# Three places in a decoder layer: squares between weight splits, twelve experts ahead in the search, running sums folded before the last group

## The reference, cut to what matters

```python
def _finish(x, mods, conv_raw, attn, ...):
    conv_y = _conv_tail(conv_raw, conv_ln_g, conv_ln_b)
    a = _rmsnorm(attn, attn_out_g)
    mix = jnp.concatenate([conv_y, a], axis=-1) @ w_out
    x = x + (1.0 + mods[2]) * mix
    h = _rmsnorm(x, norm2_g) * (1.0 + mods[4]) + mods[3]
    return x + (1.0 + mods[5]) * _peer(h, peer_wq, peer_keys, peer_u, peer_v)

def _peer(h, wq, keys, u_tab, v_tab):      # per block of tokens
    q = (tb @ wq).reshape(TOK_BLOCK, PEER_HEADS, 2, PEER_DK)
    s = jnp.einsum('thpd,hpkd->thpk', q, keys)
    sv, si = lax.top_k(s, PEER_TOPK)
    cand = sv[:, :, 0, :, None] + sv[:, :, 1, None, :]
    fv, fi = lax.top_k(cand.reshape(...), PEER_TOPK)
    eid = i1 * PEER_NKEYS + i2             # 128 x 128 experts
    g = jax.nn.softmax(fv, axis=-1)
    hid = jax.nn.gelu(jnp.einsum('td,ted->te', tb, u_tab[eid]))
    return jnp.einsum('te,ted->td', g * hid, v_tab[eid])
```

## Time and profile before

| | |
|---|---|
| median of three runs | 2441.48 us (2439.57 to 2441.72) |
| the profiled execution | 2438.12 us |
| its span of instructions | 2436.3 us |
| PE busy | 2257.6 us (93%) |
| PE weight loads busy | 1965.1 us (81%) |
| DVE busy | 1645.2 us (68%) |
| ACT busy | 925.3 us (38%) |
| POOL busy | 355.9 us (15%) |
| chain that ended last | PE 83%, DVE 7%, DMA 6%, ACT 3%, issue 1% |

### The profile page before, as it was taken

The page is one execution under the profiler, slowest core; times in us unless marked ns, Lnnn a source line. Parts: engine busy times, 40 slices in busy tenths (PEclk is TensorE's granted clock), DMA queues, the critical chain, the costliest instruction groups (busy, mean ns, idle before and its releaser), DMA issues.

```text
span 2436.3 us, 38402 instructions
## 1 busy us (share of the span) xinstructions
PE 2257.6 (93%) x14756; PEld 1965.1 (81%) x14756; DVE 1645.2 (68%) x2907; ACT 925.3 (38%) x1034; POOL 355.9 (15%) x316
## 2 busy tenths in 40 slices
PE   7699999767979988999999999999999999999986
PEld 2298888436859988988999888888888888889985
DVE  1259777324345697866888777777877777766775
ACT  0332332342243314634444343343443443444432
POOL 1043000200000004510011212222212222010000
PEclk9899999778989999999999999999999999999999
DMA  9867776766634534576777999888989889877652
GB/s 382 349 234 288 286 277 226 279 242 225 236 127 145 163 131 153 216 250 234 266 273 282 344 345 324 327 338 323 345 307 345 334 319 341 290 275 266 209 176 91
DMA packets 152112, 643.36 MB, mean 264 GB/s; under 512 B 16721, under 2 KB 17105, under 8 KB 133649
## 3 DMA queue, kind: packets, MB, share of 16 engines
q1 hardware_dynamic: 122112, 444.65, 51.8%
q0 software_dynamic: 28400, 187.90, 19.9%
q10 hardware_dynamic: 1440, 8.56, 0.8%
HBM read 618.05 MB, written 22.99 MB: 263 GB/s over the span
## 4 chain that ended last, share of the span: by engine, by line
PE 83%; DVE 7%; DMA 6%; ACT 3%; issue 1%; POOL 0%; SPq 0%; DVEq 0%; ACTq 0%
PE vb L1429 17%; PE zb L1412 15%; PE vb L1431 7%; PE zb L1414 7%; PE zb L481 6%; PE zb L483 6%; PE zb L482 6%; DMA ada_first<-in_w_ada 3%; PE zb L1374 3%; PE vb L1452 3%; PE vb L1441 2%; PE vb L1394 2%; PE vb L1102 2%; DMA cache<-in_cv 1%; PE vb L1428 1%; DVE lo L465 1%
## 5 line engine op out<-in xcount | busy, mean ns | idle before, releaser
L456 ACT ACTIVATE hi<-raw 128x1024 fp32r<-128x1024 f32 x624 | 659.5, 1059 | 1046.9 <-PE vb L1429 374.6
L465 DVE TENSOR_TENSOR lo<-raw,hi 128x1024 fp32r<-128x1024 f32 x624 | 765.3, 1229 | 359.4 <-ACT hi L456 354.8
L1412 PE MATMUL zb<-act_hl,hi 128*128 128x448 f32 x1792 | 575.6, 376 | 3.0 <-DVE lo L465 3.0
L1429 PE MATMUL vb<-w_rest,hi 128*128 128x448 f32 x1536 | 521.2, 378 | 0.0
L1414 PE MATMUL zb<-act_hl,lo 128*128 128x224 f32 x1680 | 444.7, 265 | 0.0
L481 PE MATMUL zb<-act_hl,hi 128*128 128x288 f32 x1152 | 347.2, 301 | 37.2 <-DVE act_hl L1561 37.2
L1412 PEld LDWEIGHTS zb<-act_hl,hi 128*128 128x128 f32 x1792 | 334.5, 188 | 52.3 <-issue 24.3
L1431 PE MATMUL vb<-w_rest,lo 128*128 128x224 f32 x1280 | 342.9, 268 | 0.0
L482 PE MATMUL zb<-act_hl,hi 128*128 128x288 f32 x1152 | 341.9, 297 | 0.0
L483 PE MATMUL zb<-act_hl,lo 128*128 128x288 f32 x1152 | 341.3, 296 | 0.0
L1414 PEld LDWEIGHTS zb<-act_hl,lo 128*128 128x128 f32 x1680 | 321.0, 191 | 5.0
(11 more groups left out here) (266 smaller groups left out, 2438.1 us busy)
## 6 DMA issues: line engine op xcount, KB each, us to landing
raw<-in_v SPq DMA_DIRECT2D x256, 512.0 KB, 5.3
raw<-in_u SPq DMA_DIRECT2D x224, 512.0 KB, 5.5
raw<-in_w_in SPq DMA_DIRECT2D x80, 512.0 KB, 9.4
ada_first<-in_w_ada SPq DMA_DIRECT2D x64, 512.0 KB, 8.7
ada_mid<-in_w_ada SPq DMA_DIRECT2D x64, 512.0 KB, 5.3
ada_in<-in_w_ada SPq DMA_DIRECT2D x32, 512.0 KB, 9.0
raw<-in_w_out SPq DMA_DIRECT2D x32, 512.0 KB, 4.2
ada_last<-in_w_ada SPq DMA_DIRECT2D x32, 512.0 KB, 6.9
```

What stands on the lines that cost most here:

```text
L456: act.activation(hi[s][:, :], raw[s][:, :], ACT.Copy).then_inc(hi_ready, 1)
L465: dve.tensor_tensor(lo[s][:, :], raw[s][:, :], hi[s][:, :].bitcast(F32), ALU.subtract) \
L1412: last = pe.matmul(zb[:, bank, 0:2 * ND], w_h, act_hl[:, k, :, 0:ND], start=(k == 0), stop=(k == KC - 1))
L1429: last = pe.matmul(vb[:, bank, 0:2 * ND], v_h, w[:, e % 2, :, :], start=(e == 0), stop=(e == GI - 1))
```

## The change

Three edits, each on its own stretch.

1. On ACT, the square of pair j of the output projection stands behind the first of the four splits of quad `Q_OUT` + 2 + j, and the other three behind the square. The last pair (j = 7), which has no splits, stays as it is.
2. AHEAD_TOPK is 12: six indices of `ahead` stand ahead of `turn_picks(0)`, six ahead of `turn_picks(1)`, and four (64 chunks) beside the gates.
3. The add of the two halves of `acc` becomes eight instructions of two chunks each, one in each `beside` of the U quads pp = 1 and 2 of the last body; the 16 folds into `x2` stand four by four in the `beside` of its U quad pp = 3. Nothing of them is left between the last body and the last V units.

```diff
-AHEAD_TOPK = 10
+AHEAD_TOPK = 12
...
+LAST_QUADS = 32 * (NG - 3) - 12
...
                 if j < KC // 2 - 1:
-                    quad_hi(Q_OUT + 2 + j)
+                    split_hi(act, Q_OUT + 2 + j, 0)
                 act.wait_ge(x1_tile, j + 2)
                 act.activation(hF[:, 2 * j:2 * j + 2, :], xT[:, 2 * j:2 * j + 2, :], ACT.Square).then_inc(sq_ready, 1)
+                if j < KC // 2 - 1:
+                    for s in range(1, 4):
+                        split_hi(act, Q_OUT + 2 + j, s)
...
-            for i in range(2, 5):
+            for i in range(2, AHEAD_TOPK // 2):
                 ahead_out(i)
             picks_out(0)
-            ahead_out(5)
+            ahead_out(AHEAD_TOPK // 2)
             gate_exp(1)
-            for i in range(6, AHEAD_TOPK):
+            for i in range(AHEAD_TOPK // 2 + 1, AHEAD_TOPK):
                 ahead_out(i)
...
-            for c in range(5 * KC):
+            for c in range(AHEAD_TOPK // 2 * KC):
                 ahead(c)
             turn_picks(0)
-            for c in range(5 * KC, AHEAD_TOPK * KC):
+            for c in range(AHEAD_TOPK // 2 * KC, AHEAD_TOPK * KC):
                 ahead(c)
...
+                if LAST_QUADS <= n < LAST_QUADS + 8:
+                    k = 2 * (n - LAST_QUADS)
+                    mark(dve.tensor_tensor(acc[:, k:k + 2, 0, :], acc[:, k:k + 2, 0, :], acc[:, k:k + 2, 1, :], ALU.add))
+                if n >= LAST_QUADS + 8:
+                    settle()
+                    for k in range(4 * (n - LAST_QUADS - 8), 4 * (n - LAST_QUADS - 7)):
+                        mark(dve.scalar_tensor_tensor(x2[:, k, 0:ND], acc[:, k, 0, :], m_g5[:, k, 0:1], x2[:, k, 0:ND],
+                                                      ALU.mult, ALU.add))
...
             body(NG - 2, 0)
-            mark(dve.tensor_tensor(acc[:, :, 0, :], acc[:, :, 0, :], acc[:, :, 1, :], ALU.add))
-            settle()
-            for k in range(KC):
-                mark(dve.scalar_tensor_tensor(x2[:, k, 0:ND], acc[:, k, 0, :], m_g5[:, k, 0:1], x2[:, k, 0:ND],
-                                              ALU.mult, ALU.add))
             settle()
```

## The result

The changed kernel took **2415.55 us** (median of four runs, 2413.08 to 2421.85) beside 2440.53 us for the kernel before on the same chip: a ratio of **0.9902** (95% interval 0.9886 to 0.9918), some 24 us less. The forecast was 2426.4 us with a range of 2421 to 2434: the direction is right, and the gain is larger than the range allowed. Measured a second time it took 2421.33 us (2417.61 to 2422.68), ratio 0.9925 (0.9912 to 0.9937), 18.3 us less, which is just inside that range. The nine runs together have a median of 2418.3 us, 2.7 us under its lower end.

What follows compares the result with a forecast made beforehand. TensorE, busy in 93% of the span, was taken as the bound; gains of 11.8 + 2.5 + 0.8 = 15.1 us off 2438.12 gave 2423.0 profiled, 2426.4 us with the 3.4 us median offset, range 2421 to 2434.

Steps and rivals of the forecast that it cites:

- rival B: Output projection: tile transfers keep each pair at 17.76 us, edit 1 gives only 0.2, time 2438; chance 0.07.
- the upper bound of 12.5 us for this edit: Output projection: edit 1 gains at most 12.5 us, all that TensorE's seven waits for ACT's square hold; forecast 11.8.
- The 3.4 us of the median above the profiled execution: Whole kernel: median of runs taken as 3.4 us above the profiled execution, turning 2423.0 into 2426.4 us.
- the forecast's 1020.8: Gates: with DVE as the bound, the last gate product starts at 1020.8 instead of 1023.27; net gain 2.5 us.
- Rival A: Gates: POOL's rows (sign: POOL as releaser) or slice copies come last, no speed-up; edit 2 costs 0.9, time 2429.8; chance 0.10.
- Its price, 3.4 us: Gates: up to 3.4 us of edit 2's gain lost again if DVE must still wait in later groups.
- Rival D: Gates: short waits for DVE lower the clock, 28 groups cost 151 us, time near 2496, slower than before; chance 0.02.
- what the folds find in the quad: Last U quad: 5.9 us of folds find 1.7 us of DVE idle time, so the last `w_rest` is 4.2 us late.
- Rival C: V units: folds find no idle time, 5.9 us late, clock low through unit 2; edit 3 -2.9, time 2430.1; chance 0.06.
- the delay show ahead of `w_ready`: Sign against the forecast for edit 3: the folds' delay showing in an earlier wait than `w_ready`.

Runs made afterwards that it cites:

- the filled kernel: Kernel before plus three unread TensorE products of 256 columns ahead of each of the seven waits for ACT's square in the output projection; 2434.72 us, ratio 0.9978.
- edit 1 alone: Kernel before with only the squares moved behind the first split in the output projection; 2422.73 us, ratio 0.9932.
- edit 3 alone: Kernel before with only the adds and folds moved beside the last U quads; 2437.05 us, ratio 0.9987.

## Why the prediction was right where it was, and where it failed

**The squares.** The mechanism is as forecast, to the row: the waits are gone but for one of 1.81 us at the last pair, the pair is 15.75 us (15.8 forecast), and there is no wait for a tile, which disposes of rival B. The stage is 12.4 us shorter in the two profiles, where the forecast had 11.8; the filled kernel and edit 1 alone lie 11.2 us apart by their ratios. **Here is also the step that failed**: the upper bound of 12.5 us for this edit, "all that the waits hold". A wait of TensorE can hold more than its own length. In three of four profiles the clock falls behind these waits, which costs about 1.7 us in each of three pairs, and edit 1 takes that away too: 151.1 to 152.5 us become 133.8 to 134.9, so 16 to 19 us, 17.3 in the mean. The filled kernel shows the same share in unprofiled runs, 5.4 us. I had reckoned with the clock at two places, the turn and the V units, where the row showed it low. In the projection the one profile that I read showed 1.00, and I took this execution for all of them. The 3.4 us of the median above the profiled execution may have been a sign of it. I carried them over to the kernel after as a constant, and there they were 1.6 (2415.55 less 2413.91) and, the second time, -0.7.

**The search.** DVE's wait for the second turn: 9.57 us (9.5 forecast). First gate product 3.6 us late (3.4). Gates: 80.4 us (80.2 by the forecast's 1020.8 less its shifted start), with 2.0 us of DVE's waits left:

```profile
DVE one L1919 <- PE vb L1400: 2.0, 3, 1.5
```

Net it is 2.0 us in the profiles, 2.5 forecast. Rival A's sign did come: behind the first group, TensorE's waits in the gates are put down to POOL's rows, 2.3 us in five pieces, but for one of 1.3 us for ACT's copy. Its price, 3.4 us, did not, so the sign was a poor one. Rival D did not either: with the short idle times between the groups (56.87 us busy of 60) the clock stayed at 1.00 there. So the rule on short idle times between groups of matmuls that I had cited from the Trainium skill ("TensorE: Matmul & The Clock Gate", section "A second HAM failure mode: psum-queue depth-cycling") does not show in the gates. In the projection idle times of 1.78 us were followed by the low clock in three profiles of four, and there I had not looked for it.

**The folds.** V unit 0 starts 3.5 us later behind the last U quad (4.2 forecast), unit 2 stands 7.9 us behind unit 0 (8.3) and unit 4 14.0 (14.4). So the gain is 1.9 us against the profile that I read, not 0.8. The term that was off is the one for what the folds find in the quad: 1.7 us by the named idle times, while the quad, measured from one `w_rest` to the next, grew from 10.01 to 13.14 us, 3.1 for 5.9 us of folds. An instruction behind a split that had not waited starts 1.13 to 1.14 us behind the split's start in after, though the split is recorded with 1.22: room that no named idle time shows. The gain of 1.9 us is also that of the mildest case: the profile that I read and that of the filled projection have a V stage of 62.6 us, the four others without edit 3 have 63.4 to 63.9, and against these the gain is 2.7 to 3.1 us. Rival C did not come: the clock at unit 2 is 1.00 in after (2347.5 to 2351) where it was 0.74 (2370.3 to 2376.5). Nor does the delay show ahead of `w_ready`: from the last gate product to the last U quad, edit 3 alone takes 1331.0 us and the unchanged kernel 1330.9.

**The sum.** It is 15.1 us by the forecast, 16.3 in the edited stages of the first profile, and about 17.3 + 1.7 + 2.8 = 21.8 with the stages that the kernel before has in three of four profiles. That would be 2440.5 - 21.8 = 2418.7 us, just under the range and close to the median of the nine runs, 2418.3. The two measurements gave 24 and 18. So the size of the miss in the first one is in part luck: the second lies inside the range, with the same mechanism mis-sized. The prediction also said that it is wrong if a stage with no edit changes its length by more than a microsecond. That came true by 8.3 us in the attention stage, and it was a bad sign to name: the unchanged kernel moves this stage by 5.1 us between its own two profiles. The first profile of after had the shortest such stage of all, 108.4 us, and the second had 113.6. How much of the difference between the measured 18 and 24 is chance, nine runs do not settle.

## What to carry to other kernels

A wait of TensorE costs its length, and where its clock can fall behind it, more; price a removed wait from its length upwards, and look at the duration of the first products behind it in more than one execution before calling the bound complete. Filling the wait with products that nobody reads, and timing that kernel often enough, separates the two shares. When work is moved to where an engine idles, look for the idle time behind the hand-over too (here behind the last `w_rest`, and behind the second turn): both places had room that cost nothing, and using them brought 14 us in their stages on top of the 4 of edits 2 and 3.

## What was not expected of the hardware

Idle times of the same length, 1.78 us, at the same place of the same program are followed by the low clock in one execution (2.02 us for the sum) and not in another (1.24 us). And the mean granted clock of a run, 0.962 to 0.968, goes with its time closely (2442.8 to 2432.0 us). Two medians of a handful of runs can differ by more than a small edit is worth: those of the changed kernel, of four and of five runs, are 5.8 us apart.
